# Four heads of sample attention on four 32-column strips of TensorE

## The reference

```python
def cross_attn(h, mem_k, mem_v, w_xq, w_xo):
    b, L, _ = h.shape
    q = (h @ w_xq).reshape(b, L, X_HEADS, X_HEAD_DIM)
    s = jnp.einsum('blhd,bmhd->bhlm', q, mem_k) * (X_HEAD_DIM ** -0.5)
    pr = jax.nn.softmax(s, axis=-1)
    o = jnp.einsum('bhlm,bmhd->blhd', pr, mem_v).reshape(b, L, D_MODEL)
    return o.astype(h.dtype) @ w_xo
```

## Time and profile before

| | us |
|---|---|
| median of 3 runs | 1352.07 |
| lowest and highest run | 1350.17 and 1353.94 |
| profiled execution, span from its first to its last instruction | 1353.3 |
| PE busy, share of the span | 1289.4 (95%) |
| DVE busy | 743.5 (55%) |
| ACT busy | 451.3 (33%) |
| POOL busy | 150.2 (11%) |

### The profile page before, as it was taken

How to read it: one execution, slowest core, us unless ns; L and a number is a source line. 1 busy time by engine, 2 the same in 40 slices (tenths; PEclk the granted TensorE clock), 3 DMA queues, 4 the chain that set the end, 5 groups by cost and what they waited for, 6 DMA issues and landing times.

```text
span 1353.3 us, 23876 instructions
## 1 busy us (share of the span) xinstructions
PE 1289.4 (95%) x9801; PEld 1193.5 (88%) x9801; DVE 743.5 (55%) x1484; ACT 451.3 (33%) x752; POOL 150.2 (11%) x176
## 2 busy tenths in 40 slices
PE   6999999999999898799999998899999999999996
PEld 5999988888888897689999997449999999999996
DVE  5777865656667877864344438323543443433433
ACT  4444432333332124532234323223431231322322
POOL 1000011000112957400001000001100000000000
PEclk7999989999998899999999999899999999999998
DMA  6422322222123666432233728511222222223211
GB/s 220 113 82 73 95 66 64 63 63 63 32 63 98 206 195 192 124 117 86 86 119 101 274 93 292 207 62 46 96 94 94 94 94 94 93 93 93 95 63 63
DMA packets 139214, 147.54 MB, mean 109 GB/s; under 512 B 4210, under 2 KB 132386, under 8 KB 138817
## 3 DMA queue, kind: packets, MB, share of 16 engines
q1 hardware_dynamic: 119124, 126.98, 29.3%
q10 hardware_dynamic: 18096, 8.62, 2.3%
q0 software_dynamic: 1904, 10.65, 2.2%
HBM read 130.21 MB, written 16.68 MB: 109 GB/s over the span
## 4 chain that ended last, share of the span: by engine, by line
PE 85%; DVE 8%; ACT 2%; DMA 2%; POOL 2%; issue 1%; SPq 0%; DVEq 0%; ACTq 0%
PE slot L371 67%; PE slot L1862 2%; PE aux L1624 2%; PE aux L1617 1%; PE slot L1773 1%; PE aux L1618 1%; DVE w_lo L356 1%; PE aux L1603 1%; DVE junk L1387 1%; ACT w_hi L349 1%; PE aux L1835 1%; PE slot L1853 1%; DVE sring L1199 1%; POOL win_sum L555 1%; DMA vr<-in_conv_b 1%
## 5 line engine op out<-in xcount | busy, mean ns | idle before, releaser
L356 DVE TENSOR_TENSOR w_lo<-w_raw,w_hi 128x1024 fp32r<-128x1024 f32 x186 | 234.2, 1259 | 360.9 <-ACT w_hi L349 360.8
L349 ACT ACTIVATE w_hi<-w_raw 128x1024 fp32r<-128x1024 f32 x186 | 197.0, 1059 | 571.9 <-PE slot L371 535.8
L371 PE MATMUL slot<-a_hi,w_hi 128*128 128x260 f32 x1408 | 300.8, 295 | 0.7 <-DVE a_lo L1428 0.7
L371 PE MATMUL slot<-a_hi,w_lo 128*128 128x260 f32 x1408 | 286.1, 285 | 0.0
L371 PE MATMUL slot<-a_lo,w_hi 128*128 128x260 f32 x1408 | 285.3, 285 | 0.0
L371 PEld LDWEIGHTS slot<-a_hi,w_hi 128*128 128x128 f32 x1408 | 221.5, 191 | 18.9 <-issue 15.4
L371 PEld LDWEIGHTS slot<-a_lo,w_hi 128*128 128x128 f32 x1408 | 219.9, 191 | 0.0
L371 PEld LDWEIGHTS slot<-a_hi,w_lo 128*128 128x128 f32 x1408 | 219.5, 191 | 0.0
L371 PE MATMUL slot<-b_hi,w_hi 128*128 128x260 f32 x640 | 129.0, 283 | 1.6 <-DVE gate_b L1258 1.6
L371 PE MATMUL slot<-c_hi,w_hi 128*128 128x260 f32 x640 | 129.4, 283 | 0.2 <-DVE c_lo L1340 0.2
L371 PE MATMUL slot<-b_hi,w_lo 128*128 128x260 f32 x640 | 129.0, 283 | 0.0
(11 more groups left out here) (385 smaller groups left out, 1582.4 us busy)
## 6 DMA issues: line engine op xcount, KB each, us to landing
w_raw<-in_w_in SPq DMA_DIRECT2D x32, 1024.0 KB, 5.7
w_raw<-in_w_up SPq DMA_DIRECT2D x16, 1024.0 KB, 5.3
w_raw<-in_w_down SPq DMA_DIRECT2D x16, 1024.0 KB, 5.0
sring<-in_state_ssm SPq DMA_DIRECT2D x16, 512.0 KB, 4.2
out_ssm_sample<-sring ACTq DMA_DIRECT2D x16, 512.0 KB, 3.6
w_raw<-in_w_ssd_proj SPq DMA_DIRECT2D x8, 1024.0 KB, 5.1
cache<-in_cache_mem_k SPq DMA_DIRECT2D x8, 1024.0 KB, 7.6
cache<-in_cache_mem_v SPq DMA_DIRECT2D x8, 1024.0 KB, 5.1
```

What stands on the lines that cost most here:

```text
L349: nc.scalar.activation(w_hi[:, t % 2], w_raw[:, t // 2 % 2, :, t % 2 * P:t % 2 * P + P], ACT.Copy).then_inc(hi_ready, 1)
L356: nc.vector.tensor_tensor(w_lo[:, t % 2], w_raw[:, t // 2 % 2, :, t % 2 * P:t % 2 * P + P], w_hi[:, t % 2].bitcast(F32), ALU.subtract).the ...
L371: last = nc.tensor.matmul(slot[t % 2][:, h, 0:HALF], w[:, t % 2, k, :], act[:, k, h * HALF:(h + 1) * HALF], start=(start and k == 0 and n ...
```

## The change

Head h of `values_s` writes to partitions 32 h to 32 h + 31 of one bank, which puts it on the h-th strip of 32 columns of the array, and its stationary operand has 32 columns for 8. `p_diag` is four times as large (columns 8 to 31 stay zero), and each strip starts its own sum. One copy of 128 x 256 brings all heads to `o_tok`, and two transposes of 128 x 128 take the place of eight of 8 x 128. `o_turned` and `samples` describe where head h, half j and sample b then lie, so the order in `a_hi` and `a_lo` stays the same.

```diff
-        p_diag = at("p_diag", [P, 2, NS, XH, NS], R_4 + 8192)
-        o_tok = at("o_tok", [NS, D], R_4 + 10240)
+        p_diag = at("p_diag", [P, 2, NS, XH, 32], R_4 + 8192)
+        o_tok = at("o_tok", [P, XD], R_4)
...
+        def samples(t):
+            return t[:, :, SEQ:TT].rearrange("p (h j) b -> p h j b", j=2)
+
+        def o_turned():
+            return slot[0][:, 1, XD:2 * XD].rearrange("p (j h q) -> p h j q", j=2, h=XH)[:, :, :, 0:NS]
...
-                    nc.scalar.activation(a_hi[:, :, SEQ:TT], slot[0][:, 1, 0:64].rearrange("p (k b) -> p k b", k=KT),
-                                         ACT.Copy).then_inc(o_s_hi, 1)
+                    nc.scalar.activation(samples(a_hi), o_turned(), ACT.Copy).then_inc(o_s_hi, 1)
...
-                    for j in range(2):
-                        nc.scalar.activation(o_tok[:, j * 512:(j + 1) * 512], slot[j][0:NS, 1, :], ACT.Copy).then_inc(o_s_row, 1)
+                    nc.scalar.activation(o_tok[:], slot[0][:, 1, 0:XD], ACT.Copy).then_inc(o_s_row, 1)
...
-                    nc.vector.tensor_tensor(a_lo[:, :, SEQ:TT], slot[0][:, 1, 0:64].rearrange("p (k b) -> p k b", k=KT),
-                                            a_hi[:, :, SEQ:TT].bitcast(F32), ALU.subtract).then_inc(o_s_lo, 1)
+                    nc.vector.tensor_tensor(samples(a_lo), o_turned(), samples(a_hi).bitcast(F32), ALU.subtract).then_inc(o_s_lo, 1)
...
-                    last = nc.tensor.matmul(slot[h // 2][0:NS, 1, h % 2 * XD:(h % 2 + 1) * XD], p_diag[:, m, b, h, :],
-                                            cache[n % CR][:, m, h * XD:(h + 1) * XD], start=(b == 0 and m == 0 and h % 2 == 0),
-                                            stop=(b == NS - 1 and m == 1 and h % 2 == 1), skip_group_check=True)
+                    last = nc.tensor.matmul(slot[0][32 * h:32 * h + 32, 1, 0:XD], p_diag[:, m, b, h, :],
+                                            cache[n % CR][:, m, h * XD:(h + 1) * XD], start=(b == 0 and m == 0),
+                                            stop=(b == NS - 1 and m == 1), skip_group_check=True)
...
-                    pe.wait_ge(o_s_row, 2)
-                    for k in range(KT):
-                        last = nc.tensor.transpose(slot[0][:, 1, k * NS:(k + 1) * NS], o_tok[:, k * P:(k + 1) * P], ident[0:NS, 0:NS])
+                    pe.wait_ge(o_s_row, 1)
+                    for j in range(2):
+                        last = nc.tensor.transpose(slot[0][:, 1, XD + j * P:XD + (j + 1) * P], o_tok[:, j * P:(j + 1) * P], ident[:])
```

## The result

| | before | changed |
|---|---|---|
| median, first comparison (5 runs each), us | 1352.07 | 1343.81 |
| ratio, with its 95% interval | | 0.9935 [0.9914, 0.9955] |
| median, second comparison (17 and 6 runs), us | 1352.98 | 1341.93 |
| ratio, with its 95% interval | | 0.9910 [0.9884, 0.9936] |
| span of the profiled execution, us | 1353.3 | 1343.3 |

The change is faster by 0.45 to 0.86% in the first comparison; 1342.8 was forecast. The stretch that the prediction is about became 11.29 us shorter. The span fell by 10.0 only, because the first value matmul starts 1.31 us later in this profile (851.44 against 850.13). Work that the change does not touch scatters by more than that: in the eight profiles of this document the first value matmul starts between 842.68 and 853.52.

The account below looks back on a forecast made before the run. PE was taken to bound the attention rounds, with DVE next; 5.4 + 0.5 + 1.3 + 1.5 + 0.56 = 9.3 us off the 1352.07 median gave 1342.8 us, range 1339.5 to 1352.5, drain left out.

Parts of the forecast that it names:

- The stretch that the prediction is about: Attention behind the last key product, first `values_s` to first output product: forecast to shrink from 64 to 55 us.
- The bound: Attention rounds: PE ends them now; with shorter `values_s`, DVE's 1.15 us behind `scores` becomes the end.
- plain round: Nine rounds (n=2, 3, 5, 6, 7, 9, 10, 11, 13), 3.06 us before: 0.60 us saved each, 5.4 us.
- Five turns: `values_s`: a group's eight passes overlap partly and take five turns, 1.17 us instead of 1.82; chance 0.48.
- The rival of all four strips together: `values_s`: a group takes two passes, 0.52 us, DVE ends every round; 10.7 us less, 1341.4; chance 0.12.
- n=14: Last, double group of `values_s`: 3.55 becomes 2.03 us, 1.52 saved, PE stays the bound.
- n=0 and 1: First two `values_s` groups, n=0 at the lower clock: 1.3 us saved if the clock rises when it does now.
- n=4, 8, 12: First round after each `values`, DVE held up by the subtraction to `a_lo`: 0.17 us saved each, 0.5 us.
- The end: After n=14: one `o_tok` copy for two saves 0.56 us; transposes, `a_hi` copy and subtraction change nothing.
- The sum: All attention terms: 5.4 + 0.5 + 1.3 + 1.5 + 0.56 = 9.3 us saved.
- Loads, clear, cache: Wider weight loads cost nothing; `p_diag` clear grows to about 2.1 us, harmless; cache loads start earlier.
- drain at a change of strip: Rival in `values_s`: each strip change waits, 0.163 us a matmul, 2.47 us a group; 1362 us, chance 0.12.

Follow-up runs that it names:

- second comparison: The changed kernel measured again, unaltered, beside the kernel before on one chip: 1341.93 against 1352.98 us, ratio 0.9910.
- head-by-head run: Changed kernel with round 14's double group written so that four passes for one strip follow each other: 1339.58 us in a single run.
- two-strip run: Changed kernel with heads 0 and 2 on the first strip, 1 and 3 on the second: 1344.55 against 1353.39 us, ratio 0.9950.
- the run with the maximum moved: Changed kernel with DVE's row maximum of the next tile moved behind the scaling of this one: 1335.01 against 1353.39 us, ratio 0.9872.

## Why the prediction was right, point by point

- *The bound.* Right. Reading the groups as PE time on the chain and the distance between scaling and `turn` as room gave the end of a plain round: 0.60 us of room, 0.59 us gained (3.06 to 2.47), nine times 5.3 against 5.4 forecast.
- *Five turns.* Wrong, and the step that failed. "The two of one head need the same strip and follow each other, while the first of the next head may run beside the second of the one before" took it that passes start in the order written. They don't wait for that: the changed kernel and the head-by-head run show four side by side in both orders. The rival of all four strips together, given 0.12, is what happened. It cost little in the number because the plain rounds were capped by DVE in both cases, as the two-strip run shows with its four turns.
- *n=14.* Mis-sized for that reason: 1.5 forecast, 4.79 - 2.47 = 2.32 measured; the rival's 2.3 was its size.
- *n=0 and 1.* From the first value matmul to the `turn` of round 1: 6.97 before, 856.02 - 851.44 = 4.58 after, 2.39 gained; 1.3 forecast, and 1.9 by the rival. The group at the lower clock takes 1.08 us instead of the 2.29 of five turns. Of the 2.50 us saved there the lower clock took back only 0.77, as `scores` grew from 0.95 to 1.72; the rival had priced that at half. The forecast's condition, a clock that rises when it does now, nearly held: the granted clock (stretches: us, busy by engine, granted clock, DMA share, GB/s) is 0.50 through 855 and averages 0.92 over the five microseconds behind it, so it rises near 855.8. It rose near 854.4 before, where the first value matmul stands 1.31 us earlier:

```profile
854.00:855.00 1.00, 1.00 (x6) 0.33 (x9) 0.11 (x1) 0.02 (x1) 0.00 (x0) 0.50 1.09 388
855.00:860.00 5.00, 4.25 (x36) 2.02 (x28) 2.07 (x9) 1.68 (x6) 0.00 (x0) 0.92 1.04 403
```

- *n=4, 8, 12.* 0.17 forecast; `turn` to `turn` across the `values` of head 0 went from 870.45 - 863.22 = 7.23 to 867.96 - 860.95 = 7.01: 0.22.
- *The end.* 0.56 forecast; from the `turn` of round 14 to the output product 914.36 - 911.10 = 3.26 became 904.38 - 901.72 = 2.66: 0.60. The two transposes and the copy to `a_hi` stayed beside the exponential, as said.
- *The sum.* 5.31 + 0.66 + 2.39 + 2.32 + 0.60 = 11.28 of the 11.29 us of the stretch. Forecast 9.3, by the rival 10.7. That the first median came within 1.0 us of the forecast is in part luck: the forecast was 2.0 us short in the stretch, and the scatter of the totals hid it. The median of the first comparison fell by 8.3 and of the second by 11.1, with intervals that hold both sums.
- *Loads, clear, cache.* The loads cost nothing, even eight of them within 0.16 us; the clear took 1.80 where 2.1 was said, with no one waiting; no wait for a cache load appeared. No drain at a change of strip: that rival's 2.47 us a group stands against two turns of 0.216.
- *The rules weighed.* The Trainium skill (TensorE: Matmul & The Clock Gate, "Measured speedup vs the span model") reports 2.38 times for three column strips; with four strips here the double group went from 3.55 to 1.00 us on the chain (the run with the maximum moved). That a load overlaps matmuls only of another row group (same page, "The mechanism") the runs contradict: in the changed kernel eight loads that share all 128 rows are over 0.16 us after the group began at 857.25, while its first four passes run for 0.42.

## What to carry to other kernels

Products with few output columns can share the array if each is written to its own 32-column strip, and it is the strip that counts: the same 32 columns on one strip changed nothing here. Before counting the gain, read in the timeline how far behind the shortened work the next engine finishes; here that room of 0.60 us, and not the 1.3 us saved on PE, was what a round gained, and in the plain rounds two strips did as well as four. Then look at what the new end waits for: moving DVE's row maximum out of that chain was worth another 7 us, though the same move had been worth nothing before.

## What was not expected of the hardware

Passes for different strips start side by side even when the program writes four for one strip in a row (first passes 0.013 us apart, then four more every 0.216 us). And PE's clock can fall behind a loose stretch: in the two-strip run PE was busy 0.29 and 0.42 of two microseconds, then all of the next, and from about 903 to about 906.5 the granted clock was 0.50. The first 36 rows of the output product took 5.88 us instead of 4.30 (stretches as above):

```profile
900.00:901.00 1.00, 0.29 (x4) 0.29 (x4) 0.00 (x0) 1.00 (x4) 0.00 (x0) 1.00 0.00 0
901.00:902.00 1.00, 0.42 (x6) 0.27 (x4) 0.71 (x4) 0.40 (x4) 0.00 (x0) 1.00 0.00 0
...
904.00:905.00 1.00, 1.00 (x7) 1.00 (x6) 0.00 (x0) 0.00 (x0) 0.00 (x0) 0.50 0.00 0
```

The changed kernel has nearly the same loose stretch there (0.25 and 0.40 from 902 to 904 in the first) and kept 1.00 in both of its profiles, so whether the clock falls is not fixed by the program. The kernel before is as loose at that place (0.47, 0.12 and 0.63 from 911 to 914) and kept 1.00 too, so it is not shown that the strips bring this risk. Where the clock fell, it cost about 1.6 us, behind the stretch that is compared here.
